# Four accumulator banks, three products: which loop is the outer one

## The chip, the cores and the metric

The kernel runs on one core of one Trainium2 chip. The metric is the device time of one execution in microseconds. An execution has five engines' instruction streams (TensorE, VectorE, ScalarE, GpSimd, SyncE), each in order, that meet at semaphores.

## The reference

One decoder layer on 512 tokens of width 2048, in float32: a retention branch and a spatial-gating branch, merged by sigmoid gates, and then a gated feed-forward part with a short causal convolution; RMS norms around both.

```python
h = rmsnorm(x, pre_mix_g[l])
proj = h @ w_in[l]
q, k, v, rg, su, sv, g_ret, g_sgu = jnp.split(proj, SPLIT_POINTS, axis=-1)
...
a = ret @ w_ret_proj[l]
...
bb = sgu @ w_sgu_proj[l]
merged = jax.nn.sigmoid(g_ret) * a + jax.nn.sigmoid(g_sgu) * bb
x = x + rmsnorm(merged @ w_out[l], post_mix_g[l])
h = rmsnorm(x, pre_ffn_g[l])
up = causal_depthwise_conv(h @ w_up[l], conv_w[l], conv_b[l])
gate, val = jnp.split(up, 2, axis=-1)
y = (jax.nn.gelu(gate, approximate=True) * val) @ w_down[l]
x = x + rmsnorm(y, post_ffn_g[l])
```

D_MODEL is 2048, the eight heads have width 128, D_FF is 5632.

## The kernel before

**Three products.** Every float32 operand is held as a high part and a low part of the type fp32r (`h_hi`, `h_lo`, `w_hi`, `w_lo`, `b_hi`, `b_lo`). A product of two such operands is three matmuls that add to the same PSUM bank: high by high (line 378), high stationary by low moving (line 379), low stationary by high moving (line 380). `passes` issues them. In the rows of the trace the moving operand's name stands first and the stationary one's second.

**Chunks, blocks and sides.** The weights come as one stream of chunks of 128 x 1024 values. SyncE loads a chunk into one of four slots of `w_raw`, ScalarE writes its high part (line 675), VectorE its low part (line 974) and counts `lo_ready`. `chunk` waits for it and multiplies: for each of the chunk's two k tiles (`kk`), for each of four banks (`t`), the three products of 512 columns; 24 matmuls a chunk. A *long* block is eight chunks (all of a 2048-long sum), a *short* one four, a *down* one two. A block fills the four banks of one side: side A is banks 0 to 3, side B 4 to 7.

**Handing over a bank.** In a block's first k tile each bank's first matmul waits until its former contents were read (`acc_free`, line 391 in `chunk`). In its last k tile banks 0, 1 and 2 count `acc_done` with their last matmul, and the last matmul of all counts `chunk_used`, which stands for bank 3. ScalarE or VectorE then read the banks in the order 0 to 3 (an *eviction*).

**The order of the blocks and their sides.** "Seam" stands for the place between two blocks.

- Blocks 0, 2, 4, 6 (named by their first group of four chunks), for sv and su, all on side A. Block 0 is written out by itself with `passes`, k tile by k tile; the others are `long_block`. Evictions: gelu on ScalarE (line 729) after 0 and 2, a multiply on VectorE (line 1051) after 4 and 6.
- The sgu mix: four times a long block on A and a short one on B.
- The heads: eight long blocks, all on A, in turn q/k (evicted by four copies, line 778) and value (evicted by two ScalarE instructions a bank, lines 784 and 785; the second is a Silu, before which an activation table is loaded).
- The ret mix: four times long on A, short on B (evicted by VectorE, line 1166).
- The out projection: long blocks on B, A, B, then a loop over token tiles that issues `passes` itself.
- The feed-forward part: a first gate block that is half written out (`half_chunk`, 256 columns a matmul), then for every group a gate block on A, four down blocks on B, A, B, A, and a value block on B. The gate block's banks are freed by VectorE's taps (line 1268), the down blocks' by line 1301. The last two groups' down projection ends the kernel; its last loop issues `passes` itself.

Small matmuls on side B (the attention's scores and values, lines 492 and 502; transposes, line 421) stand between the chunks of some blocks (`extra`).

Of the kernel before, what the change touches and what calls it, by code (L numbers as in the profile page):

```python
# [30 lines left out]
P = 128  # L31
# [10 lines left out]
NB = 512  # L42
# [3 lines left out]
CK = 2  # L46
# [20 lines left out]
def build_layer(nc, xT, x, w, rope, decay, mix_g, ws_t, ln_g, ln_b, b_s, post_mix_g, pre_ffn_g, conv,  # L67
                post_ffn_g, rs_dram, x2_dram, out):
    with ExitStack() as ctx:
        def sb(name, shape, dt=F32):  # L70
            return ctx.enter_context(nc.sbuf_tensor(name, shape, dt))

        def sem(name):
            return ctx.enter_context(nc.semaphore(name))
# [11 lines left out]
        w_hi = sb("w_hi", [P, RING, CK * NB], F32R)  # L86
        w_lo = sb("w_lo", [P, RING, CK * NB], F32R)
# [71 lines left out]
        ps = [ctx.enter_context(nc.psum_tensor(f"ps{i}", [P, NB], F32)) for i in range(8)]  # L159
# [11 lines left out]
        acc_done = {A: sem("acc_a_done"), B: sem("acc_b_done")}  # L171
        acc_free = {A: sem("acc_a_free"), B: sem("acc_b_free")}
# [201 lines left out]
        def _(pe):  # L374
            def passes(bank, stationary, moving, first, last, skip=False):

                (s_hi, s_lo), (m_hi_, m_lo_) = stationary, moving
                pe.matmul(bank, s_hi, m_hi_, start=first, stop=False, skip_group_check=skip)  # L378
                pe.matmul(bank, s_hi, m_lo_, start=False, stop=False, skip_group_check=skip)  # L379
                return pe.matmul(bank, s_lo, m_hi_, start=False, stop=last, skip_group_check=skip)  # L380

            def chunk(q, j, side, use, operand, kt0, first, last, tokens_out=True, skip=False):

                pe.wait_ge(lo_ready, q * RING + (j + 1))
                o_hi, o_lo = operand
                slot = j % RING
                for kk in range(CK):
                    for t in range(4):
                        if first and kk == 0 and not (isinstance(use, int) and use == 0):

                            pe.wait_ge(acc_free[side], use * 4 + (t - 3))
                        c = slice(t * P, t * P + P)
                        wide = slice(kk * NB, kk * NB + NB)
                        narrow = slice(kk * NB + t * P, kk * NB + t * P + P)
                        if tokens_out:
                            st = (o_hi[:, kt0 + kk, c], o_lo[:, kt0 + kk, c])
                            mo = (w_hi[:, slot, wide], w_lo[:, slot, wide])
                        else:
                            st = (w_hi[:, slot, narrow], w_lo[:, slot, narrow])
                            mo = (o_hi[:, kt0 + kk, :], o_lo[:, kt0 + kk, :])  # L400
                        end = last and kk == CK - 1
                        mm = passes(ps[side + t][:, :], st, mo, first and kk == 0, end, skip)
                        if end and t < 3:
                            mm.then_inc(acc_done[side], 1)

                mm.then_inc(chunk_used, 1)

            def long_block(q, side, use, extra={}, waits={}, tokens_out=True):
                for j in range(LONG):
                    if j in waits:  # L410
                        waits[j]()
                    chunk(q, j, side, use, (h_hi, h_lo), CK * j, j == 0, j == LONG - 1, tokens_out)
                    if j in extra:
                        extra[j]()

            def short_block(q, j0, side, use):
                for j in range(SHORT):
                    chunk(q, j0 + j, side, use, (b_hi, b_lo), CK * j, j == 0, j == SHORT - 1, tokens_out=False)
# [34 lines left out]
            for kt in range(DK):  # L453
                pe.wait_ge(first_w_lo if kt == 0 else lo_ready, kt // CK + 1)
                pe.wait_ge(h_lo_ready, kt + 1)
                slot, wide = kt // CK % RING, slice(kt % CK * NB, kt % CK * NB + NB)
                for t in range(TT):
                    c = slice(t * P, t * P + P)
                    mm = passes(ps[A + t][:, :], (h_hi[:, kt, c], h_lo[:, kt, c]),
                                (w_hi[:, slot, wide], w_lo[:, slot, wide]), kt == 0, kt == DK - 1)  # L460
# [79 lines left out]
            for d in range(ND - 1):  # L540
                side = (B, A)[d % 2]
# [23 lines left out]
            for t in range(TT):  # L565
# [3 lines left out]
                for j in order:  # L569
                    if t == 0:  # L570
                        pe.wait_ge(lo_ready, q * RING + j + 1)
                    for kk in range(CK):
                        kt, c, wide = CK * j + kk, slice(t * P, t * P + P), slice(kk * NB, kk * NB + NB)
                        if j < RING:
                            weights = (b_hi[:, kt, :], b_lo[:, kt, :])
                        else:
                            weights = (w_hi[:, j - RING, wide], w_lo[:, j - RING, wide])
                        mm = passes(ps[A + t][:, :], (h_hi[:, kt, c], h_lo[:, kt, c]), weights,
                                    j == order[0] and kk == 0, j == order[-1] and kk == CK - 1)
# [28 lines left out]
            def up(q, side, use):  # L608
                for j in range(LONG):
                    chunk(q, j, side, use, (h_hi, h_lo), CK * j, j == 0, j == LONG - 1, tokens_out=False)  # L610
# [27 lines left out]
            for t in range(TT):  # L638
                side, use = ((A, 53), (B, 41), (A, 54), (B, 42))[t]
                for d in range(ND):  # L640
# [3 lines left out]
                    for k in range(FT):  # L644
                        c = slice(t * P, t * P + P)
                        mm = passes(ps[side + d][:, :], (b_hi[:, FT + k, c], b_lo[:, FT + k, c]),
                                    (h_hi[:, FT * d + k, :], h_lo[:, FT * d + k, :]), k == 0, k == FT - 1)
# [802 lines left out]
```

## Time and profile before

| | |
|---|---|
| median of 3 runs | 2732.1 us (2731.69 to 2732.22) |
| the profiled execution's own time | 2731.47 us |
| its span, first to last instruction | 2729.8 us |
| TensorE busy | 2718.4 us, 12,228 matmuls and as many weight loads |
| VectorE busy | 1121.7 us |
| ScalarE busy | 786.4 us |
| GpSimd busy | 36.4 us |
| moved by DMA | 290.51 MB, mean 106 GB/s |

The span is read from one profiled execution. Matmuls are pipelined: a row's duration (0.39 us for 512 columns) is longer than the distance to the next row, so distances between starts say how fast TensorE goes, and durations don't. PEld is the weight load that belongs to each matmul and runs beside the one before.

### The profile page before, as it was taken

What the parts mean: (1) busy time and instruction counts of PE and PEld (TensorE: products, weight loads), DVE (VectorE), ACT (ScalarE), POOL (GpSimd) and SP (SyncE); (2) the same over time, 40 slices, a digit from 0 to 9 for tenths busy, and PEclk for the clock granted to TensorE, in tenths of its full rate; (3) what the DMA queues carried; (4) which work ended last, traced back from release to release, by engine and by line L of the source; (5) the groups of instructions that cost most, each with busy time, mean ns of one, the idle gap of its engine ahead of it and who ended that gap; (6) DMA issues with size and microseconds to landing.
All of it is one profiled execution on the core that took longest, in us unless ns stands there. A gap on an engine that the chain in (4) does not pass through costs nothing.

```text
span 2729.8 us, 31503 instructions
## 1 busy us (share of the span) xinstructions
PE 2718.4 (100%) x12228; PEld 2253.8 (83%) x12228; DVE 1121.7 (41%) x1296; ACT 786.4 (29%) x1010; POOL 36.4 (1%) x62
## 2 busy tenths in 40 slices
PE   9999999999999999999999999999999999999998
PEld 8888888888888888888888888888888888888887
DVE  5442323333342333436343534444444343434456
ACT  5232222223323222324331323222222222222332
POOL 0000000000000000001000000000000000000000
PEclk9999999999999999999999999999999999999999
DMA  6323233332332333444332323233232323233333
GB/s 230 98 85 101 93 100 105 111 110 87 104 111 89 93 100 98 148 129 157 116 101 93 99 92 100 87 105 95 97 100 92 100 93 99 94 98 95 97 127 128
DMA packets 78093, 290.51 MB, mean 106 GB/s; under 512 B 9120, under 2 KB 9120, under 8 KB 75728
## 3 DMA queue, kind: packets, MB, share of 16 engines
q1 hardware_dynamic: 72864, 264.28, 30.4%
q0 software_dynamic: 5168, 25.35, 2.7%
q8 instruction: 46, 0.75, 0.1%
q14 instruction: 15, 0.12, 0.0%
HBM read 277.01 MB, written 8.39 MB: 105 GB/s over the span
## 4 chain that ended last, share of the span: by engine, by line
PE 99%; ACT 0%; issue 0%; DVE 0%; DMA 0%; DVEq 0%; SPq 0%; ACTq 0%
PE ps L378 32%; PE ps L380 32%; PE ps L379 32%; PE ps L502 1%; PE ps L492 1%; PE ps L421 0%; PE ps L445 0%; DMA w_raw<-in_w 0%; DVE big L1358 0%; ACT L785 0%; ACT work L785 0%; PE ps L430 0%; ACT L729 0%; DVE h_lo L998 0%; ACT work L954 0%
## 5 line engine op out<-in xcount | busy, mean ns | idle before, releaser
L974 DVE TENSOR_TENSOR w_lo<-w_raw,w_hi 128x1024 fp32r<-128x1024 f32 x475 | 581.4, 1224 | 1378.1 <-ACT w_hi L675 1377.4
L675 ACT ACTIVATE w_hi<-w_raw 128x1024 fp32r<-128x1024 f32 x475 | 502.7, 1059 | 1612.9 <-PE ps L380 1610.6
L378 PE MATMUL ps<-h_hi,w_hi 128*128 128x512 f32 (+1 forms) x2336 | 905.0, 387 | 1.3 <-ACT work L785 1.3
L379 PE MATMUL ps<-h_lo,w_hi 128*128 128x512 f32 (+1 forms) x2336 | 902.2, 386 | 0.0
L380 PE MATMUL ps<-h_hi,w_lo 128*128 128x512 f32 (+1 forms) x2336 | 902.2, 386 | 0.0
L378 PEld LDWEIGHTS ps<-h_hi,w_hi 128*128 128x128 f32 x2336 | 438.8, 188 | 92.5 <-ACT work L785 4.3
L380 PEld LDWEIGHTS ps<-h_hi,w_lo 128*128 128x128 f32 x2336 | 438.7, 188 | 88.9
L379 PEld LDWEIGHTS ps<-h_lo,w_hi 128*128 128x128 f32 x2336 | 438.8, 188 | 87.2
L378 PE MATMUL ps<-w_hi,b_hi 128*128 128x512 f32 x640 | 249.0, 389 | 0.0
L379 PE MATMUL ps<-w_lo,b_hi 128*128 128x512 f32 x640 | 249.0, 389 | 0.0
L380 PE MATMUL ps<-w_hi,b_lo 128*128 128x512 f32 x640 | 249.0, 389 | 0.0
L378 PE MATMUL ps<-w_hi,h_hi 128*128 128x512 f32 x608 | 237.3, 390 | 0.4 <-DVE h_lo L998 0.2
L380 PE MATMUL ps<-w_hi,h_lo 128*128 128x512 f32 x608 | 236.6, 389 | 0.0
L379 PE MATMUL ps<-w_lo,h_hi 128*128 128x512 f32 x608 | 236.6, 389 | 0.0
L379 PEld LDWEIGHTS ps<-w_lo,b_hi 128*128 128x128 f32 x640 | 120.1, 188 | 25.0
L378 PEld LDWEIGHTS ps<-w_hi,b_hi 128*128 128x128 f32 x640 | 120.1, 188 | 24.9
L380 PEld LDWEIGHTS ps<-w_hi,b_lo 128*128 128x128 f32 x640 | 120.1, 188 | 24.9
L1268 DVE SCALAR_TENSOR_TENSOR work<-ps,shared,work 128x511 f32<-128x511 f32 (+1 forms) x176 | 117.9, 741 | 47.0 <-ACT work L903 47.0
L378 PEld LDWEIGHTS ps<-w_hi,h_hi 128*128 128x128 f32 x608 | 114.1, 188 | 24.6 <-issue 1.4
L380 PEld LDWEIGHTS ps<-w_hi,h_lo 128*128 128x128 f32 x608 | 114.1, 188 | 23.9
L379 PEld LDWEIGHTS ps<-w_lo,h_hi 128*128 128x128 f32 x608 | 114.1, 188 | 23.6
L1301 DVE TENSOR_TENSOR big<-ps,big 128x512 f32<-128x512 f32 x160 | 109.0, 691 | 46.3 <-PE ps L380 46.3
(155 smaller groups left out, 1401.8 us busy)
## 6 DMA issues: line engine op xcount, KB each, us to landing
w_raw<-in_w SPq DMA_DIRECT2D x487, 512.0 KB, 3.5
work<-work POOLq DMA_DIRECT2D x16, 256.0 KB, 3.3
work<-in_x POOLq DMA_DIRECT2D x4, 1024.0 KB, 7.8
x_scratch<-big POOLq DMA_DIRECT2D x4, 1024.0 KB, 5.0
big<-in_xT SPq DMA_DIRECT2D x7, 512.0 KB, 9.4
out<-big SPq DMA_DIRECT2D x3, 1024.0 KB, 3.9
work<-in_decay POOLq DMA_DIRECT2D x8, 256.0 KB, 2.9
work<-x_scratch POOLq DMA_DIRECT2D x2, 1024.0 KB, 6.7
```

Source lines behind the costliest of these rows:

```text
L378: pe.matmul(bank, s_hi, m_hi_, start=first, stop=False, skip_group_check=skip)
L379: pe.matmul(bank, s_hi, m_lo_, start=False, stop=False, skip_group_check=skip)
L380: return pe.matmul(bank, s_lo, m_hi_, start=False, stop=last, skip_group_check=skip)
L492: pe.matmul(ps[B + j][:, 0:S - j * P], qk[:, 2 * e + 1, j * P:j * P + P], qk[:, 2 * e, j * P:S], start=True, stop=True).then_inc(score_ps, 1)
L502: mm = pe.matmul(ps[B][:, i * P:i * P + P], probs[j][:, (i - j) * P:(i - j) * P + P], vrows[:, j, e * P:e * P + P], start=(j == 0), stop=( ...
L675: act.activation(w_hi[:, j, :], w_raw[:, j, :], ACT.Copy).then_inc(hi_ready, 1)
L974: TTm(w_lo[:, j, :], w_raw[:, j, :], w_hi[:, j, :].bitcast(F32), ALU.subtract).then_inc(lo_ready, 1)
L1268: STT(buf[:, t, n:S], ps[side + t][:, 0:S - n], col(t, k), buf[:, t, n:S], ALU.mult, ALU.add)\
L1301: TTm(y, bank, y, ALU.add).then_inc(acc_free[side], 1)
```

## The change

In `chunk` the loop over the three products now stands outside the loop over the four banks, and the matmul is issued there instead of through `passes`. The same 24 matmuls with the same operands are issued for a chunk. A bank's `start` flag is on its first product, its `stop` flag and its count of `acc_done` are on its third. `passes` stays in use in the four places that are written out by themselves.

```diff
--- before.py
+++ after.py
@@ -385,23 +385,25 @@
                 o_hi, o_lo = operand
                 slot = j % RING
                 for kk in range(CK):
-                    for t in range(4):
-                        if first and kk == 0 and not (isinstance(use, int) and use == 0):
-
-                            pe.wait_ge(acc_free[side], use * 4 + (t - 3))
-                        c = slice(t * P, t * P + P)
-                        wide = slice(kk * NB, kk * NB + NB)
-                        narrow = slice(kk * NB + t * P, kk * NB + t * P + P)
-                        if tokens_out:
-                            st = (o_hi[:, kt0 + kk, c], o_lo[:, kt0 + kk, c])
-                            mo = (w_hi[:, slot, wide], w_lo[:, slot, wide])
-                        else:
-                            st = (w_hi[:, slot, narrow], w_lo[:, slot, narrow])
-                            mo = (o_hi[:, kt0 + kk, :], o_lo[:, kt0 + kk, :])
-                        end = last and kk == CK - 1
-                        mm = passes(ps[side + t][:, :], st, mo, first and kk == 0, end, skip)
-                        if end and t < 3:
-                            mm.then_inc(acc_done[side], 1)
+                    end = last and kk == CK - 1
+                    wide = slice(kk * NB, kk * NB + NB)
+                    for n, (st_lo, mo_lo) in enumerate(((False, False), (False, True), (True, False))):
+                        for t in range(4):
+                            if n == 0 and first and kk == 0 and not (isinstance(use, int) and use == 0):
+
+                                pe.wait_ge(acc_free[side], use * 4 + (t - 3))
+                            c = slice(t * P, t * P + P)
+                            narrow = slice(kk * NB + t * P, kk * NB + t * P + P)
+                            if tokens_out:
+                                st = (o_lo if st_lo else o_hi)[:, kt0 + kk, c]
+                                mo = (w_lo if mo_lo else w_hi)[:, slot, wide]
+                            else:
+                                st = (w_lo if st_lo else w_hi)[:, slot, narrow]
+                                mo = (o_lo if mo_lo else o_hi)[:, kt0 + kk, :]
+                            mm = pe.matmul(ps[side + t][:, :], st, mo, start=first and kk == 0 and n == 0,
+                                           stop=end and n == 2, skip_group_check=skip)
+                            if end and n == 2 and t < 3:
+                                mm.then_inc(acc_done[side], 1)
 
                 mm.then_inc(chunk_used, 1)
```

TensorE's instructions are the only ones that change places. The first place is the end of block 2, its last k tile (psN is bank N; `w_` stands for the moving and `h_` for the stationary operand, since this block has the tokens as output rows; in block 4, below, it is the other way round). Before:

```order
L378 MATMUL ps0<-w_hi,h_hi 128x512
L379 MATMUL ps0<-w_lo,h_hi 128x512
L380 MATMUL ps0<-w_hi,h_lo 128x512
L378 MATMUL ps1<-w_hi,h_hi 128x512
L379 MATMUL ps1<-w_lo,h_hi 128x512
L380 MATMUL ps1<-w_hi,h_lo 128x512
L378 MATMUL ps2<-w_hi,h_hi 128x512
L379 MATMUL ps2<-w_lo,h_hi 128x512
L380 MATMUL ps2<-w_hi,h_lo 128x512
L378 MATMUL ps3<-w_hi,h_hi 128x512
L379 MATMUL ps3<-w_lo,h_hi 128x512
L380 MATMUL ps3<-w_hi,h_lo 128x512
```

After the change:

```order
L403 MATMUL ps0<-w_hi,h_hi 128x512
L403 MATMUL ps1<-w_hi,h_hi 128x512
L403 MATMUL ps2<-w_hi,h_hi 128x512
L403 MATMUL ps3<-w_hi,h_hi 128x512
L403 MATMUL ps0<-w_lo,h_hi 128x512
L403 MATMUL ps1<-w_lo,h_hi 128x512
L403 MATMUL ps2<-w_lo,h_hi 128x512
L403 MATMUL ps3<-w_lo,h_hi 128x512
L403 MATMUL ps0<-w_hi,h_lo 128x512
L403 MATMUL ps1<-w_hi,h_lo 128x512
L403 MATMUL ps2<-w_hi,h_lo 128x512
L403 MATMUL ps3<-w_hi,h_lo 128x512
```

Bank 0 gets its last matmul as the ninth of twelve instead of the third, bank 1 as the tenth instead of the sixth, bank 2 as the eleventh instead of the ninth; bank 3 keeps the last place.

The second place follows directly: the first k tile of block 4, on the same side. Before:

```order
L378 MATMUL ps0<-h_hi,w_hi 128x512 [waits acc_a_free,lo_ready]
L379 MATMUL ps0<-h_lo,w_hi 128x512
L380 MATMUL ps0<-h_hi,w_lo 128x512
L378 MATMUL ps1<-h_hi,w_hi 128x512 [waits acc_a_free]
L379 MATMUL ps1<-h_lo,w_hi 128x512
L380 MATMUL ps1<-h_hi,w_lo 128x512
L378 MATMUL ps2<-h_hi,w_hi 128x512 [waits acc_a_free]
L379 MATMUL ps2<-h_lo,w_hi 128x512
L380 MATMUL ps2<-h_hi,w_lo 128x512
L378 MATMUL ps3<-h_hi,w_hi 128x512 [waits acc_a_free]
L379 MATMUL ps3<-h_lo,w_hi 128x512
L380 MATMUL ps3<-h_hi,w_lo 128x512
```

After the change:

```order
L403 MATMUL ps0<-h_hi,w_hi 128x512 [waits acc_a_free,lo_ready]
L403 MATMUL ps1<-h_hi,w_hi 128x512 [waits acc_a_free]
L403 MATMUL ps2<-h_hi,w_hi 128x512 [waits acc_a_free]
L403 MATMUL ps3<-h_hi,w_hi 128x512 [waits acc_a_free]
L403 MATMUL ps0<-h_lo,w_hi 128x512
L403 MATMUL ps1<-h_lo,w_hi 128x512
L403 MATMUL ps2<-h_lo,w_hi 128x512
L403 MATMUL ps3<-h_lo,w_hi 128x512
L403 MATMUL ps0<-h_hi,w_lo 128x512
L403 MATMUL ps1<-h_hi,w_lo 128x512
L403 MATMUL ps2<-h_hi,w_lo 128x512
L403 MATMUL ps3<-h_hi,w_lo 128x512
```

The four waits for `acc_a_free` stood at the first, fourth, seventh and tenth matmul; they stand at the first four now.

## Rows read from the trace of the kernel before

**Rows 1.** The page: busy time, granted clock by slice, ending chain; issues of line 378.

```profile
PE 2718.4 (100%) x12228; PEld 2253.8 (83%) x12228; DVE 1121.7 (41%) x1296; ACT 786.4 (29%) x1010; POOL 36.4 (1%) x62
...
PEclk9999999999999999999999999999999999999999
...
PE 99%; ACT 0%; issue 0%; DVE 0%; DMA 0%; DVEq 0%; SPq 0%; ACTq 0%
...
0.00:2730.00 2730.00, 1528.31 (x3936) 739.10 (x3936) 1.00 0.33 106
```

**Rows 2.** Timeline of TensorE in a quiet stretch; columns: start us, duration us, instruction.

```profile
999.67 0.39 PE L378 MATMUL ps<-h_hi,w_hi 128*128 128x512 f32 x1
...
1000.13 0.39 PE L380 MATMUL ps<-h_hi,w_lo 128*128 128x512 f32 x1
...
1000.35 0.39 PE L378 MATMUL ps<-h_hi,w_hi 128*128 128x512 f32 x1
...
1011.91 0.39 PE L378 MATMUL ps<-h_hi,w_hi 128*128 128x512 f32 x1
```

**Rows 3.** Timeline of TensorE in `half_chunk`, matmuls of 256 columns.

```profile
1293.02 0.28 PE L380 MATMUL ps<-h_hi,w_lo 128*128 128x256 f32 x1
...
1297.93 0.28 PE L379 MATMUL ps<-h_lo,w_hi 128*128 128x256 f32 x1
```

**Rows 4.** Timeline at the first seam from a value block to the next block.

```profile
538.46 0.39 PE L380 MATMUL ps<-w_hi,h_lo 128*128 128x512 f32 x1
...
538.89 0.47 ACT L784 ACTIVATE work<-ps,rs 128x256 f32<-128x256 f32 x1 [2.28 <-PE ps L380]
...
539.37 1.28 ACT L785 ACT_TABLE_LOAD   x1
...
540.50 0.39 PE L380 MATMUL ps<-w_hi,h_lo 128*128 128x512 f32 x1
...
541.19 0.50 PE L378 MATMUL ps<-h_hi,w_hi 128*128 128x512 f32 x1 [0.30 <-ACT work L785]
...
541.39 0.48 ACT L785 ACTIVATE work<-ps,rs 128x256 f32<-128x256 f32 x1
...
541.99 0.43 PE L378 MATMUL ps<-h_hi,w_hi 128*128 128x512 f32 x1
...
543.45 0.43 PE L378 MATMUL ps<-h_hi,w_hi 128*128 128x512 f32 x1
```

**Rows 5.** Waits of the weight loads: releaser, us in total, times, longest.

```profile
PEld ps L378 <- ACT work L785: 4.3, 14, 0.7
```

**Rows 6.** Timeline at the seam after block 0.

```profile
50.40 1.28 ACT L729 ACT_TABLE_LOAD   x1 [2.35 <-PE ps L380]
...
51.70 2.42 ACT L729 ACTIVATE big<-ps,rs 128x512 f32<-128x512 f32 x4
...
52.53 0.47 PE L378 MATMUL ps<-w_hi,h_hi 128*128 128x512 f32 x1 [0.19 <-ACT big L729]
...
54.69 0.39 PE L378 MATMUL ps<-w_hi,h_hi 128*128 128x512 f32 x1
```

**Rows 7.** Timeline at the seam after block 2, ScalarE.

```profile
94.33 2.73 ACT L729 ACTIVATE big<-ps,rs 128x512 f32<-128x512 f32 x4 [2.28 <-PE ps L380]
```

**Rows 8.** Timeline at the seam after block 4.

```profile
137.42 0.39 PE L380 MATMUL ps<-h_hi,w_lo 128*128 128x512 f32 x1
...
137.92 2.66 DVE L1051 TENSOR_TENSOR big<-ps,shared 128x512 f32<-128x512 f32 x4 [1.09 <-PE ps L380]
```

**Rows 9.** Timelines at a q/k-to-value seam and at the ret mix's last seam.

```profile
493.18 2.64 ACT L778 ACTIVATE work<-ps 128x512 f32<-128x512 f32 x4 [2.28 <-PE ps L380]
...
1101.89 2.48 DVE L1166 TENSOR_TENSOR work<-ps,work 128x512 f32<-128x512 f32 x4
```

**Rows 10.** Timeline in the feed-forward loop: gate taps, first matmul of the next side-A block.

```profile
1415.33 5.36 DVE L1268 SCALAR_TENSOR_TENSOR work<-ps,shared,work 128x511 f32<-128x511 f32 x8 [2.26 <-ACT work L903]
...
1426.87 0.39 PE L378 MATMUL ps<-w_hi,b_hi 128*128 128x512 f32 x1
```

## The prediction

> **What bounds the kernel now.** I read the page's busy times first, then the chain that ended last, then TensorE's timeline in a quiet stretch, and last the timeline at the places where one block of matmuls hands its banks to the next. TensorE is busy for 2718.4 of 2729.8 us, 99% of the chain is PE, and the granted clock is full in every slice [rows 1]. So the time is the number of matmuls times their spacing, plus the few places where TensorE stands still. Busy time says nothing of the spacing, since matmuls overlap; start times do. Between 999.67 and 1011.91 lie 54 steps: 12.24 / 54 = 0.2267 us each [rows 2]. The program issues 11,808 matmuls in groups of three (3936 with line 378 [rows 1]); 460 calls of `chunk` hold 460 x 24 = 11,040 of them, and only those are re-ordered. The other four stretches (first block, token-tile loop, `half_chunk`, last loop) call `passes` still.
>
> **The steady state, which I cost at nothing.** The change makes every pair of neighbours write different banks. Before, two steps of three stay in a bank and one changes it, so the old trace holds both kinds: 999.67 to 1000.13 is two steps inside a bank (0.46), 1000.13 to 1000.35 is the step to the next bank (0.22) [rows 2]. On a display rounded to 0.01 both are 0.2267. If staying in a bank had a price, the step that leaves it would be shorter. What a step consists of can be seen from the 256-column matmuls: 1293.02 to 1297.93 is 41 steps, 0.1198 each [rows 3]; 256 columns fewer save 0.107, so a 512-column step is 0.213 of columns at the 2.4 GHz level and a fixed 0.013. The old order holds that fixed part also at the step to another bank. The other thing that moves is the stationary operand: before, the first and second product of a bank load the same one, afterwards each load differs from the one before. The page counts as many loads as matmuls, 12,228, and they are 83% busy beside them [rows 1], so a repeated operand is loaded again today, and the step after a repeated load (first to second product) is not shorter than the one after a new load. Steady state: 0.
> The Trainium skill ("TensorE: Matmul & The Clock Gate", "LDWEIGHTS" step of "Step-by-step: what each phase is for") says the load is a separate instruction so that one load can serve many matmuls, which speaks against an order that changes the operand each time. By that rule the new order would lose; here every matmul already has its load, so the row gives 0.
>
> **The seams, where the price is.** `chunk` now closes a block with banks 0 to 3 in its last four matmuls, where they used to close three apart; and it opens the next with banks 0 to 3 in its first four, where they used to open three apart. Call T the start of the block's last matmul and g = 0.2267. Bank 0 used to be complete after the matmul at T - 9g and wanted again at T + g: ten steps for its eviction if both blocks use the same side. Now it is T - 3g and T + g: four steps, 0.91 us. And the four banks are wanted at T + g to T + 4g (T + 0.91), while the four evictions run one after another on one engine. Where the sides alternate nothing is lost (below). Thirteen seams have the same side on both sides of them: after blocks 0, 2, 4 and 6 (side A), four from q/k to value, four from value to the next block (all A), and from the last short block of the ret mix to the out projection (B).
> Constants: the evictor starts 0.43 after the start of a bank's last matmul (538.46 to 538.89), and a matmul really gets going 0.16 after the end of the eviction (541.39 + 0.48 = 541.87, the matmul 541.99 and 0.04 longer than usual) [rows 4]. So after the change an eviction chain starts at T - 0.68 + 0.43 = T - 0.25, and the price of a seam is (-0.25 + four evictions + 0.16) - 0.91 = four evictions - 1.0.
> 1. Value to next block, four times. Today: bank 0's first eviction 538.89, then 1.28 of table load, TensorE starts at 541.19, 2.30 later, and goes on at the evictor's pace to bank 3 at 543.45 (2.26 more), with T = 540.50: bank 3's first matmul, the tenth of the block, at T + 2.95 [rows 4]. Afterwards: T - 0.25 + 2.30 + 2.26 = T + 4.31 for bank 3, now the block's fourth matmul; its tenth follows at + 1.36, T + 5.67. Loss 2.7, times 4 = 10.8. The waits list has this wait at 4.3 us in all today, over 14 waits [rows 5]; it is the one that grows.
> 2. After block 0: its end is not re-ordered, the start of the next is. Four gelus end at 51.70 + 2.42 = 54.12, so the fourth matmul starts at 54.28 and the tenth at 55.64; today the tenth starts at 54.69 [rows 6]. Loss 0.95.
> 3. After block 2 (gelus): these four now take 2.73 because they are paced by TensorE [rows 7]; unpaced 2.42 [rows 6]. Loss 1.4.
> 4. After blocks 4 and 6 (VectorE, line 1051): unpaced, VectorE does four such in 2.48 (line 1166), and it starts 0.50 after the matmul, not 0.43 (137.42 to 137.92) [rows 8, 9]. Loss 1.55 each, 3.1.
> 5. q/k to value, four times, copies of line 778. Paced, four take 2.64, so the last one is 2.64 - 3 x 0.68 = 0.60 [rows 9]. The gelus overlap their successor by 0.11 (0.69 each, four in 2.42 [rows 6]); I take the same, four in 2.07. Loss 1.07 each, 4.3.
> 6. Last ret mix to out projection, line 1166: four in 2.48 [rows 9]. Loss 1.5.
> Sum: 10.8 + 0.95 + 1.4 + 3.1 + 4.3 + 1.5 = 22.0 us.
>
> **What is costed at nothing, and under what cover.** Where sides alternate (the mixes, the out projection, the feed-forward loop), a block of at least 48 matmuls, 10.9 us, lies between two uses of a bank. The tightest is the gate's: its eight taps on VectorE end at 1415.33 + 5.36 = 1420.69, and side A is wanted again at 1426.87 [rows 10]; shifted by 6g = 1.36 they end at 1422.05, still 4.8 early. Without that cover it would be about 6 us a group. The engine that evicts gets to its next weight split up to 1.4 later, but the buffer of that split is wanted three chunks (16 us) on. The rotations, scores and the last tail move with TensorE and add nothing; the last loop and the tail are untouched. No wait vanishes, so nothing is gained back.
> Bounds: a cheap seam has no start-up at all (0.16 less) and copies that overlap by 0.2: -4 us in all. A dear one pays at each of four banks what the matmul at 52.53 pays, 0.28 after the eviction and 0.08 longer [rows 6]: 0.1 more at 4 x 13 banks, +5. So 18 to 27 for this mechanism.
>
> **Rivals.**
> *A same-bank turnaround is really there.* If the fixed 0.013 is the price of the bank and is only spread evenly by a queue, it goes: 11,040 x 0.0133 = 147 us, less the 22, and the kernel ends at about 2607. Against it stands that the step to another bank has it too. It decides from 22.0 / 11,040 = 2 ns a matmul on, which the rounded rows alone could hide in a pair, though not the equality over 54 steps. Chance 0.07 for a gain, large or small, that outweighs the seams.
> The Trainium skill ("TensorE: Matmul & The Clock Gate", "Back-to-back issue gap") gives N/2.4 + 2.5 ns, 215.7 for 512 columns; by it the sum would be an estimate of 121 us saved. The trace has 226.7 in either kind of step [rows 2].
> *The clock falls at the seams.* TensorE would stand nearly 2 us and then do one matmul per 0.72 us at four seams, where today it stands 0.5. If the granted clock then drops to the 1.2 GHz level for a chunk, 24 matmuls cost 0.213 more each, 5.1 us; at the four value seams +20 (2774), at all thirteen +67 (2820). For it: nothing like such a seam is in the old trace. Against: the first microseconds with their scattered work do not lower the page's row. Chance 0.06.
> The skill's same page ("A second HAM failure mode: psum-queue depth-cycling") says that cycling through banks can leave small idle times between groups that make the clock swing. No row here shows it.
> *The seams cost little.* If the evictions fit the four steps, no change: 2732. That would take four evictions in 1.0 us, and the shortest row is 0.47 for half a bank [rows 4]. Chance 0.05.
> *The mechanism above* has the rest, 0.82.
>
> **How the numbers follow.** The profiled execution took 2731.5 us, 1.7 more than its span, and the median is 0.6 above it. 2731.5 + 22.0 = 2753.5, so 2754 against the median of 2732.1. Its own range is 2750 to 2759; I widen it to 2746 and 2764 for small shifts of the steady step (1 ns is 11 us) and for the clock at one or two seams. About 0.2% (5.5 us) is what a measurement of this kernel tells from no change. Faster 0.08, the same 0.05, slower 0.87.
>
> **What would show it.** The step between matmuls stays 0.2267 inside a block. At the four value seams bank 3's first matmul starts 4.3 after T; at the other nine TensorE waits 1 to 1.5 us, on line 729, 1051, 778 and 1166's successors, lines that today cost it almost nothing. TensorE's waits grow by some 20 us, all on side A but one; the granted clock stays full. Wrong would be: a step other than 0.2267 (then the first rival, or its opposite), waits at alternating seams, or a clock below full behind a seam.

## The result, and the profile after

The changed kernel takes 2760.05 us (median of 4 runs, 2758.89 to 2761.34) against 2731.89 before (4 runs, 2731.15 to 2732.22): 28.2 us slower, a ratio of 1.0104 with a 95% interval of 1.0086 to 1.0121. The forecast was 2754, between 2746 and 2764. The profiled execution took 2761.34 us, 1.3 above its median; its span is 29.8 us longer than that of before. It was the slowest of the four, and what is read from its trace below adds up to 29.8, not to 28.2.

The page of the changed kernel, the lines that answer to [rows 1]:

```profile
span 2759.6 us, 31503 instructions
...
PE 2737.5 (99%) x12228; PEld 2259.2 (82%) x12228; DVE 1102.2 (40%) x1296; ACT 783.0 (28%) x1010; POOL 36.9 (1%) x62
...
PEclk9999999999999999999999999999999999999999
...
PE 98%; ACT 1%; DVE 0%; DMA 0%; issue 0%; SPq 0%; DVEq 0%; ACTq 0%
```

TensorE is still the bound, and the granted clock still reads 9 in every slice, which here hides something: the mean granted clock is 0.996 where it was 0.999.

TensorE's timeline inside a block of the changed kernel; a row is four matmuls of one product in four banks:

```profile
1000.80 1.07 PE L403 MATMUL ps<-h_hi,w_hi 128*128 128x512 f32 x4
1001.70 1.07 PE L403 MATMUL ps<-h_lo,w_hi 128*128 128x512 f32 x4
...
1003.52 1.07 PE L403 MATMUL ps<-h_hi,w_hi 128*128 128x512 f32 x4
```

1000.80 to 1003.52 is 12 steps, 0.2267 us each, now with every neighbour in another bank. It is the step of [rows 2]. Nothing was gained or lost there.

The weight loads' waits of the changed kernel, which answer to [rows 5]:

```profile
PEld ps L403 <- ACT work L787: 12.5, 15, 2.1
PEld ps L403 <- issue: 5.7, 7, 2.1
PEld ps L403 <- ACT work L780: 4.9, 15, 0.4
...
PEld ps L403 <- DVE big L1053: 2.3, 6, 0.4
PEld ps L403 <- ACT big L731: 2.2, 6, 0.4
...
PEld ps L403 <- DVE work L1168: 1.2, 3, 0.4
```

L787 is the Silu of line 785 before, L780 the q/k copy, L1053 and L731 the evictions of blocks 0 to 6, L1168 that of the ret mix. "issue" is the same kind of wait where the profile finds no releaser: 2.15 us at the fourth value seam, 0.5 to 0.6 at the first bank of others. Together the six rows count 52 waits, four banks at thirteen seams: so these are the thirteen seams and nothing else. No wait stands at a seam whose sides alternate.

The price of each seam can be read by subtracting the start of the same matmul, in the middle of each block, in the two traces. Between two such points the difference grows by:

| seam | forecast us | measured us |
|---|---|---|
| after block 0 | 0.95 | 0.97 |
| after block 2 | 1.4 | 1.45 |
| after blocks 4 and 6 | 1.55 each | 1.55, 1.58 |
| q/k to value, four | 1.07 each | 1.09 each |
| last ret mix to out projection | 1.5 | 1.51 |
| value to next block, four | 2.7 each | 3.95, 5.44, 4.38, 4.27 |
| everywhere else | 0 | 0.4 before the first seam, 0.0 elsewhere |

The nine seams that are not value seams are met to 0.05 us each, 11.4 us in all. The four value seams cost 18.0 instead of 10.8, and beside 0.2 us at the nine and 0.4 us at the start that is all that was missed. The 0.4 us are in the first microseconds, where the first loads land and the change touches nothing; the kernels below differ from the one before by 0.3 to 2.3 us there.

Timeline of the changed kernel at the first value seam, first TensorE's rows, then ScalarE's; it answers to [rows 4]:

```profile
547.28 0.61 PE L403 MATMUL ps<-w_hi,h_lo 128*128 128x512 f32 x2
549.55 0.49 PE L403 MATMUL ps<-h_hi,w_hi 128*128 128x512 f32 x1 [1.66 <-ACT work L787]
550.28 0.50 PE L403 MATMUL ps<-h_hi,w_hi 128*128 128x512 f32 x1 [0.24 <-ACT work L787]
551.01 1.52 PE L403 MATMUL ps<-h_hi,w_hi 128*128 128x512 f32 x2 [0.23 <-ACT work L787]
552.34 1.91 PE L403 MATMUL ps<-h_lo,w_hi 128*128 128x512 f32 x4
554.04 1.23 PE L403 MATMUL ps<-h_hi,w_lo 128*128 128x512 f32 x4
...
547.25 0.47 ACT L786 ACTIVATE work<-ps,rs 128x256 f32<-128x256 f32 x1 [3.64 <-PE ps L403]
547.73 1.28 ACT L787 ACT_TABLE_LOAD   x1
549.03 0.47 ACT L787 ACTIVATE work<-ps,rs 128x256 f32<-128x256 f32 x1
```

T, the start of the block's last matmul, is 547.28 + 0.23 = 547.51. The first eviction starts at T - 0.26, TensorE at T + 2.04, and banks 1 and 2 follow 0.73 apart, all as forecast (T - 0.25, T + 2.05, 0.72). The miss comes behind the fourth matmul: the four of 554.04 begin 1.70 after the four of 552.34, that is 0.43 a matmul, nearly twice the usual. The granted clock in the stretches around it (columns: stretch and its length, busy us and count of PE, PEld, DVE, ACT and POOL, granted clock, DMA share, GB/s):

```profile
547.90:550.90 3.00, 1.00 (x2) 0.37 (x2) 0.00 (x0) 2.99 (x7) 0.00 (x0) 1.00 0.03 12
550.90:554.30 3.40, 3.29 (x7) 2.36 (x8) 1.23 (x1) 1.74 (x4) 0.00 (x0) 0.50 0.00 0
554.30:560.00 5.70, 5.70 (x36) 5.03 (x36) 0.00 (x0) 0.00 (x0) 0.00 (x0) 1.00 0.31 95
...
653.30:660.10 6.80, 6.57 (x15) 4.75 (x15) 1.23 (x1) 1.98 (x4) 0.00 (x0) 0.50 0.24 77
```

TensorE stood for 1.66 us, then did one matmul per 0.73 us, and the clock was granted at 0.50, the 1.2 GHz level, from about the third of these on. This happened behind each of the four value seams and nowhere else but in the last microseconds, where it is low in the kernel before too. Behind the second value seam it stayed low for twice as long (the stretch from 653.30), which is why that seam cost 5.44. The other three executions of the changed kernel show a mean granted clock of 0.997, so the clock fell in them too, though for a shorter time in all.

### The profile page after: what moved, and what is told of

Read it like the earlier page. It is cut to its first block, busy times and chain, and to the rows that moved or that the text cites. A ratio compares the mean times of both kernels' runs of the same rounds, so it can differ in the third digit from the quotient of the medians.

```text
span 2759.6 us, 31503 instructions
## 1 busy us (share of the span) xinstructions
PE 2737.5 (99%) x12228; PEld 2259.2 (82%) x12228; DVE 1102.2 (40%) x1296; ACT 783.0 (28%) x1010; POOL 36.9 (1%) x62
## 4 chain that ended last, share of the span: by engine, by line
PE 98%; ACT 1%; DVE 0%; DMA 0%; issue 0%; SPq 0%; DVEq 0%; ACTq 0%
PE ps L403 91%; PE ps L378 2%; PE ps L380 2%; PE ps L379 2%; PE ps L504 1%; PE ps L494 1%; PE ps L423 0%; PE ps L447 0%; DMA w_raw<-in_w 0%; ACT L787 0%; DVE big L1053 0%; ACT work L786 0%; ACT work L787 0%; ACT big L731 0%; DVE big L1360 0%
## 5 line engine op out<-in xcount | busy, mean ns | idle before, releaser
L403 PE MATMUL ps<-h_hi,w_hi 128*128 128x512 f32 x2272 | 618.3, 393 | 10.3 <-ACT work L787 9.0
L403 PE MATMUL ps<-h_lo,w_hi 128*128 128x512 f32 x2272 | 610.5, 391 | 0.0
L403 PE MATMUL ps<-h_hi,w_lo 128*128 128x512 f32 x2272 | 609.7, 390 | 0.0
L403 PEld LDWEIGHTS ps<-h_hi,w_hi 128*128 128x128 f32 x2272 | 426.2, 188 | 106.3 <-ACT work L787 12.5
L403 PE MATMUL ps<-w_hi,b_hi 128*128 128x512 f32 x640 | 171.0, 389 | 0.0
L403 PE MATMUL ps<-w_lo,b_hi 128*128 128x512 f32 x640 | 171.0, 389 | 0.0
L403 PE MATMUL ps<-w_hi,b_lo 128*128 128x512 f32 x640 | 171.0, 389 | 0.0
L403 PE MATMUL ps<-w_hi,h_hi 128*128 128x512 f32 x512 | 142.5, 395 | 0.9 <-DVE work L1168 0.2
L403 PE MATMUL ps<-w_lo,h_hi 128*128 128x512 f32 x512 | 137.0, 389 | 0.0
L403 PE MATMUL ps<-w_hi,h_lo 128*128 128x512 f32 x512 | 136.9, 389 | 0.0
L403 PEld LDWEIGHTS ps<-w_hi,h_hi 128*128 128x128 f32 x512 | 95.8, 188 | 27.5 <-ACT work L780 4.9
```

The costliest lines, as they stand in the source:

```text
L403: mm = pe.matmul(ps[side + t][:, :], st, mo, start=first and kk == 0 and n == 0, stop=end and n == 2, skip_group_check=skip)
```

## The experiments

Each is set against the kernel before on the same chip: 2732.16 us (median of 23 runs) for runs 1 to 4, 2731.97 (15 runs) for 5 to 7.

**1. Only the inner k tiles.** Runs 1, 3 and 4 choose the order of the twelve matmuls of a k tile by a condition, here:

```diff
+                    if not end and not (first and kk == 0):
+                        seq = [(n, t) for n in range(3) for t in range(4)]
+                    else:
+                        seq = [(n, t) for t in range(4) for n in range(3)]
```

> Products outside the banks in every k tile except the first and the last of a block, which keep the old order (of the 11,040 re-ordered matmuls some 8,700 stay re-ordered). If only the seams cost, nothing is left: 2732, within 1 us, the same step of 0.2267 us and the full granted clock. If neighbouring banks themselves save or cost something per matmul, 1 ns each would be 9 us either way.

Measured: 2731.95 us (11 runs, 2731.76 to 2732.32), ratio 1.000, interval 0.9991 to 1.0009. Page and timeline of this kernel:

```profile
span 2730.5 us, 31503 instructions
```

```profile
1000.40 1.07 PE L408 MATMUL ps<-h_hi,w_hi 128*128 128x512 f32 x4
...
1008.56 1.07 PE L408 MATMUL ps<-h_hi,w_hi 128*128 128x512 f32 x4
```

1000.40 to 1008.56 is 36 steps of 0.2267. Four fifths of the re-ordered matmuls keep the new order and the time is that of before; all seams are at 0.00 by the subtraction above. The order itself costs and gives nothing; the whole effect comes from the first and last k tiles.

**2. Six in a row.** The kernel before, and in the chunks that neither open nor close a block:

```diff
+                if not first and not last:
+                    for t in range(4):
+                        for kk in range(CK):
...
+                            mm = passes(ps[side + t][:, :], st, mo, False, False, skip)
```

> The opposite of the change, on the kernel before: in the chunks that neither open nor close a block all six matmuls of a bank (two k tiles) follow each other, so five steps of six stay in a bank, not two of three. If staying in a bank costs nothing: 2732 and a step of 0.2267 us. If the fixed 13 ns of a step were the price of a bank, spread evenly, the step in these chunks would rise by 3 ns, some 18 us: 2750.

Measured: 2732.16 us (10 runs, 2731.72 to 2733.82), ratio 1.0001, interval 0.9992 to 1.0010. Its timeline inside a block:

```profile
999.76 0.39 PE L378 MATMUL ps<-h_hi,w_hi 128*128 128x512 f32 x1
...
1012.00 0.39 PE L378 MATMUL ps<-h_hi,w_hi 128*128 128x512 f32 x1
```

54 steps in 12.24 us, 0.2267 again. From no step inside a bank to five of six, the step is the same. The turnaround rival is dead in both directions.

**3. Only the last k tile of a block** (condition `end`).

> Products outside the banks only in the last k tile of a block, so that the evictions start 1.36 us later while the next block still asks for its banks three matmuls apart. Seam theory: each value seam 1.36 dearer (TensorE stands 1.8 us for bank 0 and is then no slower than the evictor), q/k 0.3, block 2 0.4, blocks 4 and 6 0.4 each, ret mix 0.4: 8 us, 2740. If the clock falls where TensorE stands for 1.8 us, up to 2 us more at each of four value seams, 2748; if it only falls when matmuls also trickle afterwards, 2740.

Measured: 2740.77 us (6 runs, 2740.53 to 2741.30), ratio 1.0032, interval 1.0020 to 1.0044. Timeline at the first value seam, and the granted clock over it:

```profile
542.11 1.07 PE L408 MATMUL ps<-w_hi,h_lo 128*128 128x512 f32 x4
544.83 0.50 PE L408 MATMUL ps<-h_hi,w_hi 128*128 128x512 f32 x1 [1.66 <-ACT work L792]
...
545.63 0.43 PE L408 MATMUL ps<-h_hi,w_hi 128*128 128x512 f32 x1
...
547.10 0.43 PE L408 MATMUL ps<-h_hi,w_hi 128*128 128x512 f32 x1
```

```profile
545.00:550.00 5.00, 5.00 (x22) 3.79 (x23) 1.23 (x1) 2.92 (x7) 0.00 (x0) 1.00 0.01 3
```

T is 542.79. TensorE stands 1.66 us, as long as in the changed kernel, starts at T + 2.04 and reaches bank 3 (547.10, the tenth matmul) at T + 4.31, 1.36 later than in [rows 4]. The clock stays full at all four value seams: a stand of this length, with a nearly full stream behind it (22 matmuls in 5.00 us), did not make it fall. q/k to value costs 0.39 once and 0.30 three times, after block 2 0.47, after blocks 4 and 6 0.55 each, the ret mix 0.44.

**4. Only the first k tile of a block** (condition `first and kk == 0`).

> Products outside the banks only in the first k tile of a block: the evictions start as early as before, but the four banks are wanted by the first four matmuls. Seam theory: value seams 1.36 dearer each (bank 3 comes at T + 2.95 as before but is now the fourth matmul), block 0 0.95, blocks 2, 4, 6 and the ret mix 0.4 each, q/k 0.3 each: 9 us, 2741. If one matmul per 0.72 us is enough to make the clock fall, up to 2 us more at each value seam, 2749. If the two halves of the change add up, this and the run with the ends give about 18 of the 28 us, the rest being what only both together cost (the starts wait for a chain that starts late).

Measured: 2743.46 us (4 runs, 2743.22 to 2743.96), ratio 1.0042, interval 1.0027 to 1.0058; 11.3 us, not 9. TensorE's timeline at the third value seam and the clock behind it:

```profile
741.92 0.39 PE L408 MATMUL ps<-w_hi,h_lo 128*128 128x512 f32 x1
742.61 0.49 PE L408 MATMUL ps<-h_hi,w_hi 128*128 128x512 f32 x1 [0.30 <-ACT work L792]
743.34 0.50 PE L408 MATMUL ps<-h_hi,w_hi 128*128 128x512 f32 x1 [0.24 <-ACT work L792]
...
744.79 0.50 PE L408 MATMUL ps<-h_hi,w_hi 128*128 128x512 f32 x1 [0.24 <-ACT work L792]
...
746.42 1.91 PE L408 MATMUL ps<-h_hi,w_lo 128*128 128x512 f32 x4
```

```profile
745.60:749.00 3.40, 3.40 (x10) 2.62 (x9) 1.23 (x1) 0.09 (x1) 0.00 (x0) 0.50 0.21 49
```

Here TensorE hardly stands (0.30 us), but banks 0 to 3 come 0.73 apart. Three value seams cost 1.40 each, as expected; the third cost 3.01, and it is the one behind which the clock fell. So the trickle with hardly a stand before it can do it, in one seam of four; that is 1.6 of the missing us. Another 0.4 is the ret mix: 0.83 instead of 0.4, because VectorE is busy with something else when bank 0 is ready (its first eviction starts at 1101.89, 0.92 before T [rows 9], where 1.61 would be free), so the chain is late before the change makes it matter.

**5. The changed kernel with the tables loaded early.**

```diff
             def leave_values(h, q):
 
+                act.activation(rt2[:, 0:1], ones[:, 0:1], ACT.Silu)
                 for t in range(TT):
...
                     act.wait_ge(sqx_ready, LONG)
+                    act.activation(rt2[:, 0:1], ones[:, 0:1], ACT.Gelu_apprx_tanh)
```

> The changed kernel, with a one-column Silu before the wait for a value block's first bank and a one-column Gelu before that of block 0, so that the activation tables are loaded while ScalarE waits. Seam theory: value seams 1.28 cheaper each (5.1 us), block 0 about 0.6. If the clock falls because of the 1.8 us stand, it stays full now, and the 7 us that it costs go too: 2747. If the trickle of one matmul per 0.72 us is enough, it still falls: 2754.

Measured: 2747.60 us (5 runs, 2747.42 to 2749.15), ratio 1.0059, interval 1.0045 to 1.0073: 12.5 us less than the changed kernel. ScalarE's and TensorE's rows at the first value seam:

```profile
542.56 1.28 ACT L785 ACT_TABLE_LOAD   x1
...
546.18 0.47 ACT L788 ACTIVATE work<-ps,rs 128x256 f32<-128x256 f32 x1 [2.13 <-PE ps L403]
...
545.76 1.07 PE L403 MATMUL ps<-w_hi,h_lo 128*128 128x512 f32 x4
547.08 0.50 PE L403 MATMUL ps<-h_hi,w_hi 128*128 128x512 f32 x1 [0.25 <-ACT work L789]
547.81 0.49 PE L403 MATMUL ps<-h_hi,w_hi 128*128 128x512 f32 x1 [0.23 <-ACT work L789]
...
549.27 0.50 PE L403 MATMUL ps<-h_hi,w_hi 128*128 128x512 f32 x1 [0.23 <-ACT work L789]
```

The table load now lies 3.6 us ahead of the eviction. TensorE stands 0.25 us and then goes at 0.73 a matmul, exactly as before; the clock is full at all four seams (mean 0.999). The value seams cost 1.33, 1.33, 1.33 and 1.31. They cost 4.51 on average in the changed kernel. The seam after block 0 costs 0.97 there and -0.08 here, 1.05 less where 0.6 was expected. Of the 3.2 saved, 1.4 are wait (2.72 in run 7 below to 1.33; the table load is 1.28 of it) and 1.8 the clock.

**6. The kernel before with the tables loaded early** (the same two lines).

> The kernel before with the same two early table loads. TensorE's waits at the four value seams (0.7 us each in all) and after block 0 (0.4) should go: 3 us, 2729. If the table load was not what TensorE waited for, 2732.

Measured: 2728.41 us (11 runs, 2728.14 to 2728.87), ratio 0.9987, interval 0.9978 to 0.9996: 3.6 us faster than before, and the fastest of all. Its timeline at the first value seam:

```profile
536.75 1.28 ACT L783 ACT_TABLE_LOAD   x1
...
539.01 0.47 ACT L786 ACTIVATE work<-ps,rs 128x256 f32<-128x256 f32 x1 [0.77 <-PE ps L380]
...
540.62 0.39 PE L380 MATMUL ps<-w_hi,h_lo 128*128 128x512 f32 x1
...
540.85 0.39 PE L378 MATMUL ps<-h_hi,w_hi 128*128 128x512 f32 x1
```

The next block starts 0.23 after the last matmul; each value seam is 0.73 cheaper than before, block 0's 0.47.

**7. The changed kernel, kept busy at the value seams.** Matmuls whose result nobody reads fill the waits: seven before the wait for bank 0, two before each of the other three.

```diff
+            def keep_going(n):
+                for _ in range(n):
+                    pe.matmul(ps[B + 3][:, :], h_hi[:, 0, 0:P], h_hi[:, 0, :], start=True, stop=True)
...
+                                if fill is not None:
+                                    if t == 0:
+                                        pe.wait_ge(prob_ready, fill * TT + TT)
+                                    keep_going(2 if t else 7)
                                 pe.wait_ge(acc_free[side], use * 4 + (t - 3))
```

> The changed kernel with matmuls that nobody reads, at the four value seams only: seven into bank 7 before the wait for bank 0 and two before each wait for banks 1 to 3, 13 in all, which fit into the time in which TensorE stands now. The waits are the same, only the idle time is filled. If the missing 7 us are the clock's: it stays full, value seams cost 2.7 instead of 4.5 each, 2753. If they have another cause (a longer wait, slower evictions), 2760 or a little above.

Measured: 2754.72 us (4 runs, 2754.05 to 2756.07), ratio 1.0083, interval 1.0067 to 1.0098; 5.3 us less than the changed kernel, with 52 matmuls more. Timeline (L384 are the added ones) and clock:

```profile
549.16 0.47 ACT L795 ACTIVATE work<-ps,rs 128x256 f32<-128x256 f32 x1 [3.64 <-PE ps L411]
...
549.64 1.75 PE L384 MATMUL ps<-h_hi 128*128 128x512 f32 x7
...
551.46 0.50 PE L411 MATMUL ps<-h_hi,w_hi 128*128 128x512 f32 x1
...
551.80 0.63 PE L384 MATMUL ps<-h_hi 128*128 128x512 f32 x2
...
553.73 0.43 PE L411 MATMUL ps<-h_hi,w_hi 128*128 128x512 f32 x1
```

```profile
549.00:554.00 5.00, 4.93 (x22) 3.41 (x21) 0.00 (x0) 4.82 (x10) 0.00 (x0) 1.00 0.19 79
```

The waits are untouched: the eviction starts at 549.16, bank 0's matmul at 551.46, 2.30 later as in [rows 4], and the four banks come 0.73 to 0.80 apart. But the clock is full, and the value seams cost 2.72, 2.72, 2.72 and 2.71, the forecast 2.7. This separates the two causes at the seams: in the profiled executions 10.9 us are waits and 7.2 of the 18.0 are the clock. The other nine seams cost 11.4 us as before. The kernels as a whole differ by only 5.3 us, because the start of this one is 1.9 us later in its trace: its first matmuls of 512 columns stand 0.43 apart up to 10.8 us, those of the changed kernel 0.23 from 6.3 us on. No added matmul stands there.

## Why the prediction was right, and where it was short

The direction and the thirteen seams were right, and 2760.05 lies in the range, but only in the widened one. The mechanism's own range was 18 to 27 us, or 2750 to 2759, and 28.2 lies above it (the waits alone, 22.3, lie inside); the range went up to 2764 for shifts of the step and for the clock at one or two seams. The clock fell at all four value seams, so "the granted clock stays full" did not hold, and "a clock below full behind a seam", named as a sign of being wrong, is there. That the total still came out inside was luck in part: the low stretches were short.

- *Steady state 0*: right. The step is 0.2267 with neighbours in different banks (changed kernel), in the same bank twice in three and five times in six. The fixed 0.013 of a step has nothing to do with banks. The prediction took a mean over 54 steps as proof that the two kinds of step are equal; such a mean mixes them and can't show it. Runs 1 and 2, which change their shares, do.
- *Another stationary operand for each matmul*: it costs nothing here. In run 1 each load of an inner k tile brings another operand than the one before, at the old step.
- *The seams*: right as a mechanism, in which thirteen they are, and in nine prices to 0.05 us. Runs 3 and 4 take the two halves apart (8.6 and 11.3 us). At the value seams, where TensorE already waited in the kernel before, the halves add up: 1.36 and 1.40 against 2.72. At the others they don't, for instance 0.47 and 0.39 against 1.45 after block 2: there the old order had slack, and each half alone still finds part of it.
- *The term that was mis-sized* is "Value to next block, four times": 2.7 forecast, 4.5 measured on average. Its wait was 2.7 (run 7). The 1.8 on top (in the profiled execution; in the median the 5.9 us that 28.2 leaves above 22.3 us of waits are about 1.5 a seam, an estimate) is the granted clock, which I had only as a rival ("The clock falls at the seams", 0.06) in place of the mechanism, priced at 5.1 a seam. It was no alternative but an addition, in the place where that rival looked for it, at a third of its price, because only some seven matmuls ran at the low level behind the first seam (x7 in the stretch from 550.90) and x15 behind the second, not 24, and a step at that level was 0.43, 0.20 more and not 0.213. The Trainium skill ("TensorE: Matmul & The Clock Gate", "A second HAM failure mode: psum-queue depth-cycling") names small idle times between groups of matmuls as a cause of a swinging clock; the trace agrees in part: 0.50 was granted behind 0.73 us steps in the changed kernel and once in run 4, but 1.00 behind the same steps in run 5. It was the warning to price the clock higher.
- *No price at alternating seams, none for weight splits, rotations and tail*: right; the differences there are 0.0.
- *Overlap of copies by 0.11*, assumed from the gelus: right, 1.09 against 1.07. Four copies take 2.06 in the changed kernel, where the forecast had 2.07:

```profile
500.45 2.06 ACT L780 ACTIVATE work<-ps 128x512 f32<-128x512 f32 x4 [3.64 <-PE ps L403]
```

What stays open is what exactly the clock needs to fall. A stand of 1.66 us alone: none of four (run 3). The trickle after 0.30: one of four (run 4). The trickle after 0.25, with the table loaded early: none of four (run 5). Both together: four of four. These are single profiled executions each. The mean granted clocks of the other executions fit: 0.997 in each of the three of the changed kernel, 0.999 or 1.0 in those of runs 3 to 5 and 7 (for run 4 too, whose profiled one has 0.998). Run 7 fills the stand and the gaps of the trickle at once, so it does not say which of the two matters.

## What to carry to other kernels

An order inside a block is free as long as TensorE's step doesn't change; it is paid where blocks meet. Count the matmuls between a bank's last use and its next first use and set them against the whole chain of evictions: staggering the last and the first k tile by bank (as the old order does) hid a four-eviction chain (all but 0.5 to 0.7 us of it where a table load stood in it, by run 6) that the new order exposed at 13 of 13 same-side seams. And if a re-ordering is wanted inside, keep the first and last k tile as they were: it then costs nothing (run 1).

An activation table load on the path of a hand-over is worth moving even in a tuned kernel: two added lines of code, which run five times in all on one column, gave 3.6 us on the kernel before.

## What was not expected of the hardware

A granted clock of 0.50 followed waits of under 2 us with four single matmuls behind them, inside a stream that is otherwise dense for 2.7 ms, and in the profiled execution it added 1.8 us on average to a price of 2.7. The slice row of the page does not show it; the mean granted clock (0.996 for 0.999) and the stretches behind the waits do.
